# Delta-rule branch of a hybrid decoder kernel: dense products between the small ones in two column halves

## What is computed

```python
def token_mixer(h, ...):
    proj = (h @ p['w_in'][l]).astype(f32)
    p_ret, p_gla, p_rwkv, p_merge = split_cols(proj, ...)
    y_ret, sr = retention_branch(p_ret, ...)
    y_gla, sg = gla_branch(p_gla, ...)
    y_rw, sw, ss = rwkv7_branch(p_rwkv, ...)
    gates = jax.nn.sigmoid(p_merge).reshape(B, T, N_BRANCH, D_MODEL)
    merged = (gates[:, :, 0] * (y_ret @ wb[0]) + gates[:, :, 1] * (y_gla @ wb[1])
              + gates[:, :, 2] * (y_rw @ wb[2]))
    out = merged.astype(h.dtype) @ p['w_out'][l]

def rwkv7_scan(r, w, k, v, kk, a, S0):
    def step(S, xs):
        sa = jnp.einsum('bhvk,bhk->bhv', S, -kk_t)
        S = S * w_t[:, :, None, :] + sa[..., None] * (kk_t * a_t)[:, :, None, :] + v_t[..., None] * k_t[:, :, None, :]
        y = jnp.einsum('bhvk,bhk->bhv', S, r_t)
```

## Time and profile before

| | |
|---|---|
| median of 3 runs | 2682.39 us (2680.4 to 2683.08) |
| profiled execution, its own time | 2682.8 us |
| its span, first to last instruction | 2681.0 us |
| mean granted TensorE clock | 0.997 |
| PE busy | 2618.6 us, 98% of the span |
| DVE, ACT busy | 846.6 us (32%), 580.6 us (22%) |
| delta-rule branch, layer 0 | from about 416 to 744 us |
| delta-rule branch, layer 1 | from about 1501 to 1829 us |

### The profile page before, as it was taken

How to read it: one execution, slowest core, us unless ns; L and a number is a source line. 1 busy time by engine, 2 the same in 40 slices (tenths; PEclk the granted TensorE clock), 3 DMA queues, 4 the chain that set the end, 5 groups by cost and what they waited for, 6 DMA issues and landing times. The chain is left out here.

```text
span 2681.0 us, 79189 instructions
## 1 busy us (share of the span) xinstructions
PE 2618.6 (98%) x34890; PEld 2130.0 (79%) x34890; DVE 846.6 (32%) x2419; ACT 580.6 (22%) x1731; POOL 0.2 (0%) x4
## 2 busy tenths in 40 slices
PE   8999999999999999999999999999999999999998
PEld 5777887777777777677778777777799999999997
DVE  2022665555511000102266555562311111111111
ACT  2222333323211000112333323321111111111111
POOL 0000000000000000000000000000000000000000
PEclk9999999999999999999999999999999999999999
DMA  6333342222233434342354222223499999999997
GB/s 220 114 127 131 131 154 82 77 66 71 87 133 123 137 134 140 104 141 73 119 179 153 92 66 71 78 95 107 154 390 387 369 380 395 375 370 382 392 368 276
DMA packets 145537, 498.98 MB, mean 186 GB/s; under 512 B 18736, under 2 KB 23472, under 8 KB 142800
## 3 DMA queue, kind: packets, MB, share of 16 engines
q1 hardware_dynamic: 145360, 496.43, 51.0%
HBM read 476.07 MB, written 20.29 MB: 185 GB/s over the span
## 5 line engine op out<-in xcount | busy, mean ns | idle before, releaser
L301 PE MATMUL psum<-hT,ring 128*128 128x288 f32 x2088 | 570.1, 413 | 0.0
L301 PEld LDWEIGHTS psum<-hT,ring 128*128 128x128 f32 x2088 | 375.9, 190 | 92.5 <-ACT work L403 2.7
L392 PE MATMUL psum<-work,ring 128*64 128x88 f32 x11264 | 435.0, 239 | 3.5 <-issue 3.5
L392 PEld LDWEIGHTS psum<-work,ring 128*64 128x64 f32 x11264 | 433.2, 136 | 6.2 <-issue 5.7
L2142 PE MATMUL psum<-work,proj 128*64 128x88 f32 x5632 | 223.5, 239 | 0.2 <-issue 0.2
L2142 PEld LDWEIGHTS psum<-work,proj 128*64 128x64 f32 x5632 | 218.2, 136 | 4.8 <-issue 4.8
L385 PE MATMUL psum<-hT,ring 128*128 128x288 f32 x768 | 187.1, 407 | 0.0
L1433 ACT ACTIVATE work<-psum 128x256 f32<-128x256 f32 (+4 forms) x304 | 102.5, 371 | 390.3 <-PE psum L1344 100.6
L385 PEld LDWEIGHTS psum<-hT,ring 128*128 128x128 f32 x768 | 146.0, 190 | 40.7 <-issue 0.8
L1858 PE MATMUL psum<-hT,ring 128*128 128x288 f32 x704 | 172.6, 409 | 1.7 <-DVE hT L1937 1.7
L1858 PEld LDWEIGHTS psum<-hT,ring 128*128 128x128 f32 x704 | 135.0, 192 | 39.4 <-issue 2.1
(11 more groups left out here) (444 smaller groups left out, 3026.1 us busy)
## 6 DMA issues: line engine op xcount, KB each, us to landing
ring<-w_ff_dram SPq DMA_DIRECT2D x420, 512.0 KB, 6.6
ring<-w_mix_dram SPq DMA_DIRECT2D x256, 512.0 KB, 3.6
proj<-w_ff_dram SPq DMA_DIRECT2D x128, 512.0 KB, 5.3
proj<-w_ff_dram SPq DMA_DIRECT2D x64, 384.0 KB, 5.5
work<-s_gla_dram SPq DMA_DIRECT2D x8, 1024.0 KB, 5.3
gla_s_out<-work SPq DMA_DIRECT2D x8, 1024.0 KB, 4.6
work<-s_ret_dram SPq DMA_DIRECT2D x8, 512.0 KB, 4.8
ret_s_out<-work SPq DMA_DIRECT2D x8, 512.0 KB, 3.0
```

The costliest lines, as they stand in the source:

```text
L301: mm = nc.tensor.matmul(out, ring[:, s, k, :], rhs[:, k, :], start=(k == 0), stop=(k == KT - 1))
L392: mm = nc.tensor.matmul(out[64 * c:64 * c + 64], ring[:, s, k, 64 * c:64 * c + 64], rhs[:, k0 + k, :], start=(k0 + k == 0), stop=(k0 + k = ...
```

## The change

In the delta-rule branch alone, `side` is built with `narrow=True`. Each dense product of 128 x 128 weights becomes two products of 128 x 64 weights, one for each half of the output features. They lie in the two column halves of the array, write partitions 0 to 63 and 64 to 127 of the same bank, and stream the same 288 tokens. The six products at L822 stay whole, and so do those of the two other users of `Between`. The order of the steps is kept, and so are the waits; `slab_done` is raised by the second half of the last product.

```diff
+    def in_halves(out, weights, x, start, stop):
+
+        for c in range(2):
+            last = nc.tensor.matmul(out[64 * c:64 * c + 64], weights[:, 64 * c:64 * c + 64], x, start=start, stop=stop)
+        return last
+
     class Between:
-        def __init__(self, slabs, begun=0):
+        def __init__(self, slabs, begun=0, narrow=False):
+            self.narrow = narrow
             self.products = self.emit(slabs, begun)

         def emit(self, slabs, begun):
             for n, (wait, s, out, rhs) in enumerate(slabs):
                 wait()
                 for k in range(begun if n == 0 else 0, KT):
-                    mm = nc.tensor.matmul(out, ring[:, s, k, :], rhs[:, k, :], start=(k == 0), stop=(k == KT - 1))
+                    mm = (in_halves if self.narrow else nc.tensor.matmul)(
+                        out, ring[:, s, k, :], rhs[:, k, :], start=(k == 0), stop=(k == KT - 1))
                     if k == KT - 1:
                         mm.then_inc(slab_done, 1)
                     yield
...
-                           + [(lambda n=n: out_wait(n), ...) for n in range(OUT_EARLY)], begun=SIDE_BEGUN)
+                           + [(lambda n=n: out_wait(n), ...) for n in range(OUT_EARLY)], begun=SIDE_BEGUN, narrow=True)
```

More of the change, by code:

```diff
@@ L1139, in _ @@
                             for i in range(KT) for j in range(4)]
-                           + [(lambda n=n: out_wait(n), n, SIDE_BANK[n][:, 0:T], hT) for n in range(OUT_EARLY)], begun=SIDE_BEGUN)
+                           + [(lambda n=n: out_wait(n), n, SIDE_BANK[n][:, 0:T], hT) for n in range(OUT_EARLY)], begun=SIDE_BEGUN, narrow=True)
             def lora_up(i):
```

## The result

The changed kernel takes 2689.14 us (median of 12 runs, 2687.65 to 2690.32). The kernel before takes 2682.16 us beside it (12 runs, 2679.61 to 2684.12). The ratio is 1.0028 with a 95% interval of 1.0021 to 1.0036, so the change costs 0.28% (the medians differ by 7.0 us). The span of the profiled execution is 2687.1 us, with a mean granted clock of 0.998.

The account below looks back on a forecast made before the run. PE was taken to bound the kernel. Tile changes of 2.71 us a layer, 5.4 in two, made 5.9 with slots; on the profiled 2682.8 that is 2688.7, less 0.4 for the median: 2688.3 us, range 2684 to 2693.5.

Parts of the forecast that it names:

- The pace of halves: Delta-rule dense products: two halves go through at once, keeping 0.243 us a slot; slots lose 0.5 us in all.
- The entries and exits: Around dense runs: from 64 x 64 gains 0.048 us, from whole-array work costs 0.152, exit into `key_norm` or `bonus_sum` 0.20.
- What waits swallow: Before the second level and around `bonus_sum`, PE's waits for DVE (0.58 and 0.42 us) hide the tile-change costs.
- rival in which no wait swallows anything: Delta-rule branches: all entries and exits count, 10.9 us with the slots, 2693.3 us; chance 0.08.
- last pair: Last pair of a delta-rule branch: one entry of 0.152 paid, seven gains of 0.048 kept, -0.18 us.
- The branch: Each layer's delta-rule branch takes 2.71 us more, before the term for slots.
- stretch ahead of the loop: Delta-rule branch before its loop: three entries of 0.152 and two exits of 0.20, 0.86 us.
- rival in which it had spare time: Waits swallow more, ahead of the loop in both layers and in the first pair: 4.0 us stay, 2686.4; chance 0.11.
- first pair: First pair of a delta-rule branch: its second level waits less, 0.08 us spare, so 0.35 us is paid.
- Equal columns, no change of tile size: Delta-rule pairs: only columns set the price, entries from 64 x 64 gain 0.19, 2637 to 2660 us; chance 0.06.
- Weight loads not hidden: Dense slots: a half's weight load can't run under the other product, 0.05 us a slot, 53 us, 2735; chance 0.03.

Follow-up runs that it names:

- second experiment: Changed kernel with column halves only in dense runs having whole-array work on at least one side, the others whole: 2693.84 us against 2681.67 for the kernel before.
- first experiment: Changed kernel with column halves only in dense runs having 64 x 64 products on both sides, the others whole: 2676.99 us against 2681.67 for the kernel before.
- third experiment: Changed kernel with halves only before the second level (from the second pair on) and before `bonus_sum`: 2682.06 us against 2681.67 for the kernel before.
- fourth: Changed kernel with the halves on rows 0 to 63 alone, 64 x 64 tiles, half of each dense sum left out: 2757.24 us against 2681.67 before.
- sixth experiment: Kernel before, with delta-rule dense products from the third slab on as 64 x 64 quarters of two slabs together, full sums: 2648.44 us against 2681.88.

## Why the prediction was right

**The pace of halves.** Right: 0.242 us a slot before and after, in the first `side(6)`. The term for it (0.5 ns a slot, 0.25 us a branch) is not found. `side(14)` ahead of the loop starts at 425.10 before and at 426.11 after, so up to the first `scores` it takes 6.88 and 6.94 us. The 0.06 are the longer first record and the second half's delay (0.052 + 0.007), and for its 28 slots nothing is left, within 0.4 ns each.

**The entries and exits.** Right: from a transpose into halves 0.14 by the rows above, or 0.15 with the second half's delay (forecast 0.152), 0.20 from halves into `key_norm` (0.20), and in the gated-linear branch 0.20 into the whole array and 0.05 less into halves. The second experiment bears the count out: four entries of 0.152 with one exit of 0.20, less one gain, give 0.76, measured 0.75. In the first experiment ten gains of 0.048 would give -0.48, and -0.42 was measured. When the records of the pair are laid beside those of before, each of the ten gains is 0.045 to 0.048, and 0.047 is lost again at `scores_rest`, as shown there. The changed kernel loses it too. So a pair's entries and exits come to 0.29 (forecast 0.280), and the rest up to 0.33 is this one gain. The forecast had not listed a wait there.

**What waits swallow.** Right, and shown alone for the two places of the third experiment: they cost 0.00 us a pair. The rival in which no wait swallows anything (2693.3) falls with it. In the last pair both waits of `level_x` for ACT are gone, as said. That pair was to gain 0.18 and gains 0.11.

**The branch.** The forecast of 2.71 and about 0.25 for slots is 2.96; it took 3.05. The stretch ahead of the loop holds 0.82 (0.86 forecast), so the rival in which it had spare time (2686.4) falls too. Up to the first `variance` come 0.50 more: the first pair (0.35), and the first two levels of the second pair (0.152 - 0.048 = 0.10), for `variance(0)` stands there.

So the mechanism was right, and the sum came out within 0.1 us a branch partly by luck, since its errors cancel: 0.25 for slots and 0.04 ahead of the loop weren't there, and 0.33 of gains lost at `scores_rest` in seven pairs and 0.07 in the last pair weren't counted.

**Equal columns, no change of tile size.** Wrong, as judged: entries from 64 x 64 into 128 x 64 are paid, for they gain 0.046 and not 0.19. The fourth and the sixth experiment show that this rival had the right size for the case it described: where the dense work has both the rows and the columns of the small products, 2.4 to 3.1 us a pair come back (3.2 by its formula). The Trainium skill, "TensorEngine Tiling (Array Packing)", section Key Properties, draws the line between modes, and not at columns; the traces agree at each border that they show.

**Weight loads not hidden.** Wrong, as judged: it would have cost 53 us.

The total, 2689.14, lies 0.8 above the forecast of 2688.3. The branches account for 6.1 of the 7.0 us between the medians. The other 0.9 is less than the runs of either kernel spread (2.7 and 4.5 us), and less than the 2 us by which two executions differ outside the branches; it isn't explained.

## What to carry to other kernels

A product is not dear or cheap by its own shape alone: each change of tile size that was priced here costs 0.14 to 0.20 us on TensorE by the tile that comes in, so read both neighbours of every run, and what waits there already, before splitting it. Filler between small products is best given the small products' own tile, by running row halves of two sums side by side, so that nothing is recomputed or lost in pace. And a stage's price can be read beforehand from borders elsewhere in the same trace, if the end of a record is corrected by how early it lets its successor in.

## What the runs showed of the hardware

Four 64 x 64 float32 products with 288 tokens, in the four quarters of the array and from two different sums, keep the pace of one whole product: 16 records in 1.20 us. What the array does in the 0.14 to 0.20 us of a change of tile size, these runs don't tell.

In the kernel with dense products on rows 0 to 63 alone the granted clock was 1.00, the level of 2.4 GHz, until 424 us, and then 0.50, that of 1.2 GHz, for 34 us, with PE busy throughout. In the view by windows the columns after the window are its length, busy time and records of PE, PEld, DVE, ACT and POOL, the granted clock, DMA's share and GB/s:

```profile
416.00:424.00 8.00, 7.19 (x50) 3.44 (x50) 5.68 (x23) 3.11 (x7) 0.00 (x0) 1.00 0.33 99
424.00:458.00 34.00, 33.21 (x286) 21.31 (x287) 9.70 (x31) 5.68 (x16) 0.00 (x0) 0.50 0.16 48
```

Ahead of the fall PE had made ten such dense products and idled for 0.81 us, waiting for ACT. From 458 us on it was 1.00 again for the rest of the branch. At the head of the branch of layer 1 it fell once more: 1.00 up to 1502.7 us, and then 0.50 for 27 us, with PE busy for 26.5 of them. It doesn't happen in every execution: of the four, three have a mean granted clock of 0.984 to 0.987, and the fastest (2727.85 us) has 0.998. In the changed kernel, in the same stretch with all rows in use, it was 1.00:

```profile
424.00:458.00 34.00, 32.71 (x462) 20.19 (x462) 17.36 (x52) 13.04 (x31) 0.00 (x0) 1.00 0.28 87
```

That a busy engine was given half the clock was not expected; what of its work decides it, these runs don't tell. In the sixth experiment, with the same tiles on all rows, the mean granted clock was 0.998.
